# GLA and RW take their input without the norm's root; VectorE multiplies by the root at each eviction

## What is computed

```python
def rmsnorm(x, g):
    x32 = x.astype(jnp.float32)
    y = x32 * lax.rsqrt(jnp.mean(x32 * x32, axis=-1, keepdims=True) + EPS)
    return (y * g.astype(jnp.float32)).astype(x.dtype)
...
    h = h + conv_ffn(rmsnorm(h, norm_ffn[i]), ffn_w_up[i], ffn_dw[i], ffn_w_down[i])
...
    z = h @ w_in                       # here h is rmsnorm(h, norm_mix[1])
    z_gla, z_rw = z[..., :GLA_COLS], z[..., GLA_COLS:]
...
    q, k, v, go, glr = jnp.split(z_gla, _splits(GLA_SIZES), axis=-1)
...
    zr = zr + (token_shift(zr) - zr) * rw_mu
```

## Time and profile before

| what | us |
|---|---|
| median of the timed runs | 3647.69 |
| lowest and highest of 3 | 3642.44, 3647.90 |
| span of the profiled execution (slowest core, the only one) | 3632.3 |
| PE busy in that span | 3508.2 |
| DVE busy | 2358.6 |
| ACT busy | 1848.1 |
| mean granted clock of PE | 0.990 |

### The profile page before, as it was taken

The page is one execution under the profiler, slowest core; times in us unless marked ns, Lnnn a source line. Parts: engine busy times, 40 slices in busy tenths (PEclk is TensorE's granted clock), DMA queues, the critical chain, the costliest instruction groups (busy, mean ns, idle before and its releaser), DMA issues.

```text
span 3632.3 us, 76714 instructions
## 1 busy us (share of the span) xinstructions
PE 3508.2 (97%) x29352; PEld 3427.2 (94%) x29352; DVE 2358.6 (65%) x3501; ACT 1848.1 (51%) x2670; POOL 307.0 (8%) x363
## 2 busy tenths in 40 slices
PE   8989999999999999999999999999998999999998
PEld 7989999999999898888889999999997999999998
DVE  5987666657665634666656666567767657756555
ACT  4655555444444534444435555444565445475443
POOL 2761200000000000000004000000022000000000
PEclk9999999999999999999999999999999999999999
DMA  5545565565655543222125666666565555556675
GB/s 159 167 143 162 166 177 173 173 189 174 174 173 175 165 131 111 59 59 65 53 60 171 175 174 178 196 182 180 166 187 144 163 161 165 163 151 186 194 195 146
DMA packets 1103744, 561.77 MB, mean 155 GB/s; under 512 B 23044, under 2 KB 1101462, under 8 KB 1103526
## 3 DMA queue, kind: packets, MB, share of 16 engines
q1 hardware_dynamic: 1102309, 554.58, 53.6%
q0 software_dynamic: 624, 2.13, 0.2%
q10 hardware_dynamic: 608, 2.23, 0.2%
HBM read 556.77 MB, written 2.10 MB: 154 GB/s over the span
## 4 chain that ended last, share of the span: by engine, by line
issue 64%; PE 21%; DVE 6%; POOLq 3%; DVEq 3%; ACT 2%; SPq 1%; POOL 0%; ACTq 0%; DMA 0%
PE ps L359 5%; PE ps L360 5%; PE ps L361 5%; DVE w_lo L327 2%; PE ps L443 2%; PE ps L445 2%; PE ps L444 2%; POOLq L489 2%; DVEq L679 1%; DVE arena L860 1%; POOLq L938 1%; ACT w_hi L321 1%; DVE arena L682 1%; DVEq L854 1%; ACT arena L643 0%
## 5 line engine op out<-in xcount | busy, mean ns | idle before, releaser
L327 DVE TENSOR_TENSOR w_lo<-raw,w_hi 128x1024 fp32r<-128x1024 f32 (+1 forms) x1136 | 1351.5, 1206 | 709.3 <-ACT w_hi L321 699.4
L321 ACT ACTIVATE w_hi<-raw 128x1024 fp32r<-128x1024 f32 (+1 forms) x1136 | 1132.9, 1014 | 481.3 <-PE ps L445 248.8
L359 PE MATMUL ps<-x_hi,w_hi 128*128 128x272 f32 (+1 forms) x2816 | 804.1, 286 | 1.4 <-DVE w_lo L327 1.4
L360 PE MATMUL ps<-x_lo,w_hi 128*128 128x272 f32 (+1 forms) x2816 | 802.8, 285 | 0.0
L361 PE MATMUL ps<-x_hi,w_lo 128*128 128x272 f32 (+1 forms) x2816 | 802.8, 285 | 0.0
L443 PE MATMUL ps<-x_hi,w_hi 128*128 128x256 f32 (+2 forms) x2512 | 714.5, 284 | 43.5 <-DVE w_lo L327 27.7
L444 PE MATMUL ps<-x_lo,w_hi 128*128 128x256 f32 (+2 forms) x2512 | 705.7, 281 | 0.0
L445 PE MATMUL ps<-x_hi,w_lo 128*128 128x256 f32 (+2 forms) x2512 | 705.4, 281 | 0.0
L359 PEld LDWEIGHTS ps<-x_hi,w_hi 128*128 128x128 f32 x2816 | 533.7, 190 | 3.4 <-DVE w_lo L327 3.1
L361 PEld LDWEIGHTS ps<-x_hi,w_lo 128*128 128x128 f32 x2816 | 533.8, 190 | 0.0
L360 PEld LDWEIGHTS ps<-x_lo,w_hi 128*128 128x128 f32 x2816 | 533.7, 190 | 0.0
(11 more groups left out here) (552 smaller groups left out, 5399.9 us busy)
## 6 DMA issues: line engine op xcount, KB each, us to landing
raw<-ffn_w_up SPq DMA_DIRECT2D x352, 512.0 KB, 4.3
raw<-w_in SPq DMA_DIRECT2D x232, 512.0 KB, 3.7
raw<-cd_w_in SPq DMA_DIRECT2D x100, 512.0 KB, 3.6
raw<-ffn_w_down SPq DMA_DIRECT2D x128, 384.0 KB, 3.4
raw<-ab_w_in SPq DMA_DIRECT2D x80, 512.0 KB, 3.8
raw<-ffn_w_down SPq DMA_DIRECT2D x128, 320.0 KB, 3.3
raw<-w_out SPq DMA_DIRECT2D x48, 512.0 KB, 4.1
raw<-ab_w_out SPq DMA_DIRECT2D x32, 512.0 KB, 4.0
```

Of the source, the lines that this page charges most:

```text
L321: nc.scalar.activation(w_hi[:, j % SLOTS, 0:kt], raw[:, j % RING, 0:kt], ACT.Copy).then_inc(rounded, 1)
L327: nc.vector.tensor_tensor(w_lo[:, j % SLOTS, 0:kt], raw[:, j % RING, 0:kt], w_hi[:, j % SLOTS, 0:kt].bitcast(F32), ALU.subtract).then_inc( ...
L359: nc.tensor.matmul(acc, w_hi[:, j % SLOTS, k, 0:w], mh, start=first, stop=False)
L360: nc.tensor.matmul(acc, w_hi[:, j % SLOTS, k, 0:w], ml, start=False, stop=False)
```

## The change

ACT and DVE make `xm_hi` and `xm_lo` as gain times `h`, without the root, tile by tile inside the loop of `down01`, right behind the square (ACT) and around the addition (DVE). The meeting `ffn0` is gone, with the multiplication by the root that stood behind it. PE runs the two parts of `glr` first (each k-tile waits for its own low part) and the sum for the root after them. ACT takes the root into `m_root` in SBUF, and DVE multiplies by it at each eviction: `glr`, `k`, `q` and `v` from PSUM to SBUF; `go` in place in PSUM, after which ACT applies Silu; `rw` in place, then DVE also scales by 1 - mu and adds the shifted part, with drains in between. ACT no longer evicts these tiles. POOL waits for both banks of the last down results where it met the others. `m_root` lies in free space behind the RW temporaries, `z_tap` goes, and `end_tensor` counts `norm_xn` from 4 in place of 8, since one norm less adds to it.

```diff
+    m_root, _ = place("m_root", [P, T], F32, x_off + 8 * DK * T + 4 * (1024 + T))
...
-    MEETINGS = order("ffn0", "out")
+    MEETINGS = order("out")
...
@@ -657,6 +658,8 @@
                     two_squares(act, i, u // 2)
                 else:
                     square_tile(act, name2, i, u // 2, 2, 0)
+                    nc.scalar.activation(tile_of(xm_hi, u // 2, i, 2), tile_of(h, u // 2, i, 2), ACT.Copy,
+                                         scale=col("norm_mix", i * 2 + (DK + u // 2))).then_inc(norm_hi[2], 1)
         run_phase(act, ph[name2], squares if f else None, round_part)
 
     def ffn_vector(dve, layer, f):
@@ -697,6 +700,12 @@
         name2 = f"down{layer}{f}"
         p2 = ph[name2]
 
+        def low_mid(i, s):
+
+            dve.wait_ge(norm_hi[2], i * 2 + (s + 1))
+            nc.vector.scalar_tensor_tensor(out=tile_of(xm_lo, s, i, 2), in0=tile_of(h, s, i, 2), scalar=col("norm_mix", i * 2 + (DK + s)),
+                                           in1=tile_of(xm_hi, s, i, 2).bitcast(F32), op0=ALU.mult, op1=ALU.subtract).then_inc(norm_lo[2], 1)
+
         def low_input(i, s):
 
 
@@ -706,15 +715,15 @@
                                            op0=ALU.mult, op1=ALU.subtract).then_inc(x0_lo_made, 1)
 
         def add(i, u):
-            if u == 2 and layer and f:
-                low_input(i, 0)
+            if u == 2 and f:
+                (low_input if layer else low_mid)(i, 0)
             if u % 2:
                 result_ready(dve, p2, i, u)
                 t = tile_of(h, u // 2, i, 2)[:, META * layer:T]
                 nc.vector.tensor_tensor(t, ps[:, bank(name2, u // 2), 0:T - META * layer], t, ALU.add).then_inc(drained[bank(name2, u // 2)], 1)
-            if u == 3 and layer and f:
+            if u == 3 and f:
                 dve.drain()
-                low_input(i, 1)
+                (low_input if layer else low_mid)(i, 1)
         run_phase(dve, p2, add, split_part)
 
     def ffn_tensor(pe, layer, f):
@@ -1740,9 +1749,15 @@
         p, m = (t - 2) // 3, (t - 2) % 3
         return (8, 0, 16)[m] + p, (lanes[p % 2].k, lanes[p % 2].r, lanes[p % 2].v)[m]
 
+    go_rooted = sem("go_rooted")
+
+    def mid_root(act):
+
+        nc.scalar.activation(eps[:, 10:11], eps[:, 3:4], ACT.Abs_reciprocal_sqrt)
+        act.wait_ge(norm_sum, 3)
+        nc.scalar.activation(m_root[:], ps[:, 2, 0:T], ACT.Abs_reciprocal_sqrt, bias=eps[:, 0:1], scale=1.0 / D).then_inc(norm_std, 1)
+
     def mid_scalar(act):
-        keep = {"k": 4, "q": 0, "v": 8}
-
         def work(u):
             name, t = what(u)
             if name in ("o", "y"):
@@ -1752,24 +1767,11 @@
                         square_tile(act, "cd_out", 0, k, 2, TAIL)
                         input_high(act, 1, k)
                 return
-            result_ready(act, ph["mid"], 0, u)
-            acc, free = ps[:, bank("mid", u), 0:T], drained[bank("mid", u)]
             if name == "glr":
-                nc.scalar.activation(g_low, ps[0:META, bank("mid", u), 0:T], ACT.Copy).then_inc(free, 1)
+                mid_root(act)
             elif name == "go":
-                nc.scalar.activation(zg[:, 16 + t], acc, ACT.Silu).then_inc(free, 1)
-            elif name == "rw":
-                tile, z = mid_rw(t)
-                p, m = (t - 2) // 3, (t - 2) % 3
-                if p >= 2:
-                    lane, done_ = lanes[p % 2], (p // 2 - 1)
-                    if m < 2:
-                        act.wait_ge(lane.ev, done_ * len(EDGE_V) + EDGE_V["ready"])
-                    else:
-                        act.wait_ge(lane.bt, done_ * len(BODY_T) + BODY_T["p42"])
-                nc.scalar.activation(z, acc, ACT.Copy, scale=ommu[:, tile:tile + 1]).then_inc(z_tap, 1)
-            else:
-                nc.scalar.activation(zg[:, keep[name] + t], acc, ACT.Copy).then_inc(free, 1)
+                act.wait_ge(go_rooted, t + 1)
+                nc.scalar.activation(zg[:, 16 + t], ps[:, bank("mid", u), 0:T], ACT.Silu).then_inc(drained[bank("mid", u)], 1)
         upto = stream(act, "mid", round_part, work)
 
         def low():
@@ -1782,12 +1784,35 @@
         upto(len(ph["mid"].parts))
 
     def mid_vector(dve):
+        keep = {"k": 4, "q": 0, "v": 8}
+
         def work(u):
             name, t = what(u)
             acc, free = ps[:, bank("mid", u), :], drained[bank("mid", u)]
-            if name == "rw":
+            if name == "glr":
+                dve.wait_ge(norm_std, 3)
+                result_ready(dve, ph["mid"], 0, u)
+                nc.vector.tensor_tensor(g_low, acc[0:META, 0:T], m_root[0:META], ALU.mult).then_inc(free, 1)
+            elif name in keep:
+                result_ready(dve, ph["mid"], 0, u)
+                nc.vector.tensor_tensor(zg[:, keep[name] + t], acc[:, 0:T], m_root[:], ALU.mult).then_inc(free, 1)
+            elif name == "go":
+                result_ready(dve, ph["mid"], 0, u)
+                nc.vector.tensor_tensor(acc[:, 0:T], acc[:, 0:T], m_root[:], ALU.mult).then_inc(go_rooted, 1)
+            elif name == "rw":
                 tile, z = mid_rw(t)
-                dve.wait_ge(z_tap, t + 1)
+                p, m = (t - 2) // 3, (t - 2) % 3
+                result_ready(dve, ph["mid"], 0, u)
+                nc.vector.tensor_tensor(acc[:, 0:T], acc[:, 0:T], m_root[:], ALU.mult)
+                if p >= 2:
+                    lane, done_ = lanes[p % 2], (p // 2 - 1)
+                    if m < 2:
+                        dve.wait_ge(lane.ev, done_ * len(EDGE_V) + EDGE_V["ready"])
+                    else:
+                        dve.wait_ge(lane.bt, done_ * len(BODY_T) + BODY_T["p42"])
+                dve.drain()
+                nc.vector.tensor_scalar(z, acc[:, 0:T], ommu[:, tile:tile + 1], None, ALU.mult)
+                dve.drain()
                 nc.vector.scalar_tensor_tensor(out=z[:, 1:], in0=acc[:, 0:T - 1], scalar=col("cd_rw_mu", tile), in1=z[:, 1:],
                                                op0=ALU.mult, op1=ALU.add).then_inc(free, 1)
                 dve.drain()
@@ -1808,10 +1833,12 @@
                 if t == 0:
                     pe.wait_ge(cd_lo, k // 4 + 1 if name == "o" else k + 3)
                 return (buf[:, k, 0:CD_W] for buf in ((xm_hi, xm_lo) if name == "o" else (yc_hi, yc_lo)))
-            if u == 0 and k % 4 == 0:
-                pe.wait_ge(norm_lo[2], k // 4 + 1)
+            if u == 0:
+                pe.wait_ge(norm_lo[2], k + 1)
             return xm_hi[:, k, 0:T], xm_lo[:, k, 0:T]
         upto = stream_tensor(pe, "mid", operand, 1)
+        upto(2)
+        norm_tensor(pe, 2, 0, "down01")
         weave(upto, gla_tensor(pe), edge_tensor(pe, 0), edge_tensor(pe, 1), body_tensor(pe, 0), body_tensor(pe, 1))
         upto(len(ph["mid"].parts))
 
@@ -2770,8 +2797,6 @@
             root_scalar(act, 0)
             for f in range(2):
                 ffn_scalar(act, 0, f)
-            meet(act, "ffn0")
-            norm_scalar(act, 2, 0, True, "down01", hi=xm_hi)
             mid_scalar(act)
             root_scalar(act, 1)
             for f in range(2):
@@ -2790,8 +2815,6 @@
             dve.wait_ge(norm_std, 2)
             for f in range(2):
                 ffn_vector(dve, 0, f)
-            meet(dve, "ffn0")
-            norm_vector(dve, 2, 0, lambda k: col("norm_mix", DK + k), hi=xm_hi, lo=xm_lo)
             mid_vector(dve)
             dve.wait_ge(norm_std, 4)
             for f in range(2):
@@ -2808,8 +2831,6 @@
             norm_tensor(pe, 1, 0, "ab_out")
             for f in range(2):
                 ffn_tensor(pe, 0, f)
-            meet(pe, "ffn0")
-            norm_tensor(pe, 2, 0, "down01")
             mid_tensor(pe)
             norm_tensor(pe, 3, TAIL, "cd_out")
             for f in range(2):
@@ -2821,20 +2842,18 @@
 
         @block.gpsimd
         def _(pool):
-
-            behind = {
-                "ffn0": lambda: (mid_pool(pool), level_pool(pool), sum_two(pool), two_pool(pool)),
-            }
             start_pool(pool)
             for b in range(2):
                 pool.sem_inc(sq_used[b], 1)
             ab_pool(pool)
             sum_squares(pool, "ab_out", 0)
             sum_squares(pool, "down01", 0)
-            for name in MEETINGS:
-                meet(pool, name)
-                if name in behind:
-                    behind[name]()
+            phases_out(pool, "mid")
+            mid_pool(pool)
+            level_pool(pool)
+            sum_two(pool)
+            two_pool(pool)
+            meet(pool, "out")
 
 
 def kernel(**inputs):
```

More of the change, by code:

```diff
@@ L2636, in end_tensor @@
             j, k0 = b // 4, 4 * (b % 4)
-            pe.wait_ge(norm_xn, 4 * 2 + b % 4 + 1)
+            pe.wait_ge(norm_xn, 4 + b % 4 + 1)
             for k in range(4):
```

2 lines of the change are left out of this document (1 added, 1 removed).

## The result

| | before | after |
|---|---|---|
| median of 5 runs each, us | 3647.69 (3640.68 to 3648.47) | 3627.18 (3621.93 to 3634.38) |
| ratio, 95% interval | | 0.9948 (0.9934 to 0.9961) |
| span of the profiled execution | 3632.3 | 3622.8 |

(The ratio is taken over all the runs; the two medians alone give 0.9944.) The two profiled executions, however, differ by 9.5 us.

The account below looks back on a forecast made before the run. PE, busy 97% of the span, was taken as the bound. The terms -10.8 - 2.4 + 3.2 sum to -10.0 us, so the median of 3647.7 us was to become 3637.7, with a range of 3630 to 3648.

Parts of the forecast that it names:

- The seam: Between the first FFN's last down matmul and the first full-weight matmul, PE's idle and half-clock time goes: 10.8 us gained.
- The down stage and GLA's evictions: Extra ACT and DVE work in the last down stage and 25 GLA evictions moved to DVE are covered: cost 0.
- The first pair: At the first RW pair ACT's chain no longer stands behind an eviction, so PE starts 2.4 us earlier.
- The pairs: In the later RW pairs 1.06 us more DVE time per eviction outruns cover at two places a period: 3.2 us lost.
- DVE as the bound: Rival: in the RW chains all extra DVE time counts, +14.4 us in total, 3662 us; chance 0.05.
- Half of that: Rival: RW loses 6 to 20 us as delays move PE's interleaved work; at 13.8 us, 3648 us; chance 0.22.
- more than forecast: Rival: the clock stays up at the first pair and RW loses nothing, -15.7 us, 3632 us; chance 0.08.
- A stall in the seam's place: Rival: PE still waits 2 us for POOL's sum before the norm matmul, -8.0 us, 3639.7 us; chance 0.05.
- the 5 us by which the runs of before differ: Taken, with the small terms' bounds, as the spread of the forecast for the whole kernel's measured time.
- the 15.4 us between the profiled span and the median: Whole kernel: span 3632.3 against median 3647.7; what lies around the span was claimed to be untouched by the change.
- The sentence that 0.2% is about what a measurement can tell: Whole kernel: about 0.2% (7.3 us) was claimed to be what a measurement can tell from no change.

Follow-up runs that it names:

- b_evict_cut: Kernel before, ended behind the first model's second mixer, with only the GLA and RW evictions moved to DVE (multiplying by ones), seam unchanged: 1985.4 us.
- a_cut: Changed kernel, ended behind the first model's second mixer, nothing else altered: 1974.6 us.
- b_cut: Kernel before, ended behind the first model's second mixer, nothing else altered: 1985.5 us.
- b_again: Whole kernel before, repeated unchanged with a profile: 3643.3 us, ratio 0.9999 to the reference runs of the same kernel.
- a_again: Whole changed kernel, repeated unchanged: 3634.2 us against 3642.6 of the kernel before, ratio 0.9983.
- a_once_more_cut: Changed kernel, ended behind the first model's second mixer, scaling by 1 - mu done twice at each RW eviction: 1986.2 us.
- a_twice: Whole changed kernel with the scaling by 1 - mu done three times in place of once at each RW eviction: 3667.6 us.
- a_two_ops: Whole changed kernel with RW evictions of two DVE operations in place of three: 3631.1 us, ratio 0.9961 to the kernel before.
- a_two_ops_cut: Changed kernel with RW evictions of two DVE operations in place of three, ended behind the first model's second mixer: 1970.1 us.
- a_meet_cut: Changed kernel with the four engines' meeting back at the seam, ended behind the first model's second mixer: 1979.6 us.

## Why the prediction was right and wrong

- **The seam**: forecast -10.8. Right: 17.4 us became 6.4 (-11.1), at PE's sums for the GLA output -10.8 (the start of line 1108's matmuls, 206.6 us behind the last addition, 195.7 at line 1117), and 10.8 us between b_evict_cut and a_cut. No idle time, full clock, the low part 2.9 us early as worked out.
- **The down stage and GLA's evictions**: forecast 0. Right; PE is busy 80 of 80 us, and b_evict_cut has PE's sums for the GLA output at the same distance as b_cut, 206.6 us.
- **The first pair**: forecast -2.4. Right: from line 1108 to line 1481 it took 26.4 us (1399.40 to 1425.83), now 23.9 (1387.55 to 1411.47), -2.5. The wait is 4.95 where I had said 4.5.
- **The pairs**: forecast +3.2, with 0.34 and 0.20 us a period. Right: 0.58 against 0.54 a period, and the cover read from the earlier trace rows predicts three other loads within 0.1 us. From the first pair to the last result the traces of before and after give -10.5 + 10.8 + 2.5 = +2.8. It is luck that they come so near: b_again and a_again give -7.5 + 13.3 = +5.8, since the clock fell a second time in a_again (3.7 us).
- **The rivals**: DVE as the bound did not come; its point, 20.5 us lost (0.79 per eviction), lies between a_once_more_cut (9.9 us by the trace on top of the change's own 2.8) and a_twice (29.3 on top of it). Half of that, 6 to 20 us, did not come either (2.8 to 5.8). Nor did more than forecast: the clock didn't stay up at the first pair, it was at half for about 7 us where it had been for 10. A stall in the seam's place did not come, but I had priced it too low: with a wait of 2.4 us ahead of the norm matmul it cost 4.2 to 4.6, not 2, since the clock fell behind it. The kernel before showed this already: its clock was still full in 1195.5 to 1196 and at half from 1196 on the earlier trace rows, behind one gap of 2.46 us and the first 0.4 us of the next.
- **The step that failed** is the last: what the sum was set against, and how wide the answer is. I took the median of the first runs of before as its time, put "the 5 us by which the runs of before differ" as its spread, and read the 15.4 us between the profiled span and the median as lying around the span. The first median of before lay 3.6 us above the pooled one, that of after 7.2 us below. Runs showed 1.7 to 1.8 us around the span, a spread of 24 us and more from one execution to the next, and a true difference of 9.7 us (whole, pooled) or 10.9 us (cut) that the first comparison gave as 20.5. The sizes of the sum were right; the range of the measured time was too narrow by what five executions leave open. The sentence that 0.2% is about what a measurement can tell was as optimistic: the first comparison missed the pooled value by 0.3%.

## What to carry to other kernels

Price extra work on a helper engine against the idle time behind it at each place, not by its share of the span: 0.5 us more at each of three evictions cost nothing, 1.1 us cost 0.6 and 2.2 us cost 2.9 a period of 55. Pull a norm's root out of the critical chain where the product is linear in it, and put the sum for it behind work that needs no other engine: the wait can cost twice, once as idle time and once as half clock behind it. And where one span and a median differ by more than the few us around a span, ask first how far executions of the same program lie apart; cutting the program behind the change turns a spread of 24 us and more into one of 2 to 13, but for single executions 20 to 30 us late.

## What the runs showed of the hardware that I had not expected

- PE has more than one pace at full granted clock, with no wait between the matmuls. In the second model's last stage it is 885 or 852 matmuls in 100 us (3.9%). In the first model's FFN fourteen traces had one pace, and a_two_ops and a_two_ops_cut a slower one (1581 against 1624 in 200 us, 2.7%), which made their last addition of down01 come at 1212 us in place of 1192. It seems to belong to the execution and not to the kernel: the trace of a_two_ops_cut is of its one execution of 1991.2 us, and the other five took 1966.6 to 1974.6. That also explains this late execution; the one of a_cut has no trace. Below, after and a_two_ops. What chooses the pace stays open.

```profile
800.00:1000.00 200.00, 200.00 (x1624) 200.00 (x1623) 139.01 (x200) 96.06 (x133) 0.00 (x0) 1.00 0.63 178
```

```profile
800.00:1000.00 200.00, 200.00 (x1581) 200.00 (x1580) 134.56 (x191) 93.24 (x127) 0.00 (x0) 1.00 0.62 177
```

- A gap of 2.37 us in PE's work was enough for the granted clock to go to half (0.61 in 1194 to 1196, 0.54 in the two us after), though PE worked again when it fell; it was full again from 1198 on. But it isn't enough every time. At the first norm of the program all 16 traces have the same gap of 2.03 or 2.04 us, with PE busy at full clock in the 10 us ahead of it: in 11 of them the clock stayed full, in 5 it fell behind the gap. Below, the three us behind it in before and in b_again. At the end of the cut kernels a gap of 3.1 us left the clock full in four traces (a_cut, a_meet_cut, b_cut, b_evict_cut) and brought half in four. The Trainium skill, "TensorE: Matmul & The Clock Gate", section Why this matters for your kernels, advises idle gaps of no more than about 3 us; here the measurement decides, and by it shorter gaps are at risk too.

```profile
409.00:412.00 3.00, 3.00 (x24) 2.91 (x25) 0.01 (x1) 2.96 (x5) 0.33 (x1) 1.00 0.19 57
```

```profile
409.00:412.00 3.00, 3.00 (x15) 3.00 (x15) 1.09 (x1) 1.87 (x2) 0.00 (x0) 0.50 0.00 0
```

- A multiplication in place in PSUM (128x272) takes 0.44 to 0.45 us, hardly more than the one from PSUM to SBUF (0.43 to 0.44), and an operation with descending addresses takes 0.50 us like the ascending one.
